# How the probabilities of the windowed attention are turned on TensorE in a hybrid block: by an fp32r copy and one-pass transposes, with q's and k's transposes as ordinary products

## The reference

```python
hn = rms_norm(h, mix_norm_g)
rq, rk, rv, rg, sq, sk, sv, gr, gs = split(hn @ w_in)
y_ret = rms_norm(retention(rq, rk, rv)) * silu(rg)
y_swa = sliding_window_attention(sq, sk, sv, q_norm_g, k_norm_g, sinks)
merged = sigmoid(gr) * (y_ret @ w_ret_branch) + sigmoid(gs) * (y_swa @ w_swa_branch)
h = h + merged @ w_out
h = h + square(relu(rms_norm(h, mlp_norm_g) @ w_up)) @ w_down
```

```python
scores = q @ keys.T - slopes * dist          # 128 x 272 a head and block
m = maximum(max(scores), sink)
p = exp(scores - m)
probs = p / (sum(p) + exp(sink - m))
y = probs @ vals
```

## Time and profile before

| what | us |
|---|---|
| median of three runs | 1619.83 |
| lowest and highest | 1619.79, 1620.44 |
| span of the profiled execution, first to last instruction | 1618.2 |
| median less that span | 1.6 |
| TensorE busy (share of the span) | 1610.1 (99%) |
| VectorE busy | 1030.6 (64%) |
| ScalarE busy | 769.9 (48%) |
| GpSimd busy | 437.1 (27%) |

### The profile page before, as it was taken

One profiled execution on the slowest core, in us unless ns is written; L12 is line 12 of the kernel. 1 busy time (PEld: TensorE's weight loads), 2 busy tenths in 40 slices (PEclk: granted clock), 3 DMA queues, 4 the chain that ended last, 5 costly groups with the idle time before them and its releaser, 6 DMA issues.

```text
span 1618.2 us, 22594 instructions
## 1 busy us (share of the span) xinstructions
PE 1610.1 (99%) x7984; PEld 1347.5 (83%) x7984; DVE 1030.6 (64%) x1913; ACT 769.9 (48%) x1567; POOL 437.1 (27%) x675
## 2 busy tenths in 40 slices
PE   9999999999999999999999999999999999999999
PEld 6888888888888888888888888888888888888887
DVE  6775556655657676757565338866665657766675
ACT  6533334545547676763222126655545544444442
POOL 1101010221359888875221000121111122100000
PEclk9999999999999999999999999999999999999999
DMA  8323232645424343438553223344444399733452
GB/s 289 116 98 117 95 124 72 232 166 186 162 88 114 84 94 83 106 82 262 164 202 104 72 65 124 129 170 150 149 144 148 119 321 356 239 98 98 149 183 92
DMA packets 119599, 236.53 MB, mean 146 GB/s; under 512 B 13904, under 2 KB 48128, under 8 KB 119488
## 3 DMA queue, kind: packets, MB, share of 16 engines
q0 software_dynamic: 45904, 126.93, 23.6%
q1 hardware_dynamic: 73440, 108.03, 21.6%
q10 hardware_dynamic: 144, 0.13, 0.0%
HBM read 157.05 MB, written 69.47 MB: 140 GB/s over the span
## 4 chain that ended last, share of the span: by engine, by line
PE 97%; DVE 1%; DMA 1%; ACT 0%; SPq 0%; POOL 0%; issue 0%; DVEq 0%; ACTq 0%
PE bank L1084 29%; PE bank L1089 29%; PE bank L1088 29%; PE bank L1370 2%; PE bank L1402 2%; PE bank L1384 2%; PE bank L1419 0%; PE bank L1127 0%; PE bank L1502 0%; PE bank L1288 0%; PE bank L1406 0%; PE bank L1452 0%; DMA PX<-in_w_in 0%; PE bank L1387 0%; DVE WL L2172 0%; PE bank L1427 0%
## 5 line engine op out<-in xcount | busy, mean ns | idle before, releaser
L1084 PE MATMUL bank<-WH,ADH 128*128 128x512 f32 x448 | 174.3, 389 | 0.0
L1088 PE MATMUL bank<-WH,ADL 128*128 128x512 f32 x448 | 174.3, 389 | 0.0
L1089 PE MATMUL bank<-WL,ADH 128*128 128x512 f32 x448 | 174.3, 389 | 0.0
L1084 PE MATMUL bank<-HN,WH 128*128 128x512 f32 x384 | 152.4, 397 | 0.0
L2098 ACT CAST ADH<-ARAW 128x512 fp32r<-128x512 f32 x112 | 69.5, 621 | 169.9 <-PE bank L1089 160.9
L1089 PE MATMUL bank<-HN,WH 128*128 128x512 f32 x384 | 150.3, 391 | 0.0
L1088 PE MATMUL bank<-HN,WL 128*128 128x512 f32 x384 | 150.0, 391 | 0.0
L959 POOL TENSOR_SCALAR PR<-PR,RC 128x272 f32<-128x272 f32 (+1 forms) x128 | 131.0, 1099 | 44.9 <-DVE RC L2663 44.4
L2917 DVE TENSOR_TENSOR ADL<-ARAW,ADH 128x512 fp32r<-128x512 f32 x112 | 77.5, 692 | 96.9 <-ACT ADH L2098 96.7
L1084 PE MATMUL bank<-SOPH,WH 128*128 128x512 f32 x256 | 99.8, 390 | 0.0
L1089 PE MATMUL bank<-SOPL,WH 128*128 128x512 f32 x256 | 99.6, 389 | 0.0
(11 more groups left out here) (356 smaller groups left out, 4242.8 us busy)
## 6 DMA issues: line engine op xcount, KB each, us to landing
ARAW<-uop SPq DMA_DIRECT2D x112, 256.0 KB, 3.0
uop<-US POOLq DMA_DIRECT2D x64, 256.0 KB, 2.8
WRAW<-in_w_up SPq DMA_DIRECT2D x15, 1024.0 KB, 6.2
RAW<-in_w_in SPq DMA_DIRECT2D x58, 256.0 KB, 4.0
gates<-TB POOLq DMA_DIRECT2D x48, 256.0 KB, 2.4
uop<-UA POOLq DMA_DIRECT2D x48, 256.0 KB, 3.1
proj<-SA POOLq DMA_DIRECT2D x36, 256.0 KB, 2.5
RT<-proj POOLq DMA_DIRECT2D x8, 1024.0 KB, 8.8
```

The costliest lines, as they stand in the source:

```text
L1084: mm = pe.matmul(bank, ahi, bhi, start=first, stop=False, skip_group_check=onto)
L1088: pe.matmul(bank, alo, bhi, start=False, stop=False, skip_group_check=onto)
L1089: return pe.matmul(bank, ahi, blo, start=False, stop=last, skip_group_check=onto)
```

## The change

- A new tile PW (fp32r, two buffers of 128 x 544) takes a copy of the pair's probabilities. SP makes it by a DMA (`copy_p`), which waits until GpSimd has scaled the pair (pn_rdy) and the pair before the last in this buffer is turned.
- The turn reads PW with IDR, an fp32r transpose instead of an fp32 one (what the change calls one-pass), and comes a step later: LAG = 3 instead of 2, STEPS 68 instead of 67. The values move from even to odd steps.
- q's and k's turns, in the loop and ahead of it, are no transposes any more but ordinary products with IDR. In the loop they are no longer a group behind P's turn: each stands by itself between two of the last gate products of its step (`turn_next`, through a callback `between` in `three`), so ahead of the values, P's turn and the scores.
- The sinks are written by VectorE at the head of `top`, which now waits for the copy of pair T - 3 and not for its turn.
- PW takes room: KV holds four token blocks instead of eight, K/V are loaded later, and the two aside weight blocks have a tile of their own (RAWA). Loads of weight blocks 2, 3, 6 and 7 are issued two steps later; those that follow blocks 0 and 1 stay.

```diff
+LAG = 3
-STEPS = NPAIR + 3
+STEPS = NPAIR + LAG + 1
...
+        PW = at("PW", O_M + 12288, [2, 2 * NKEY], F32R)
...
+            def copy_p(pair):
+
+                n, b = pair // 8, pair % 2
+                lo, hi = (0, 2 * NKEY) if n else (P, P + 2 * NKEY0)
+                sp.wait_ge(pn_rdy, pair + 1)
+                if pair >= 2:
+                    sp.wait_ge(pt_full, pair - 1)
+                sp.dma_start(PW[:, b, lo:hi].bitcast(F32), PR[:, pair % 3, 1 + lo:1 + hi]).then_inc(pw_full[b], 16)
+
             for T in range(STEPS):
+                if 2 <= T < NPAIR + 2:
+                    copy_p(T - 2)
+                if T >= LAG + 2 and T % 2 == 1:
+                    G = (T - LAG - 2) // 2
+                    sp.wait_ge(ya_rdy, G + 1)
+                    for par in range(2):
+                        sp.dma_start(y_place(G, par), y_part(G, 0, par)).then_inc(yc_done[G % 2], 16)
...
                 for slab, k in new_slabs(T):
                     if slab < SLAB_E and k in (0, 1):
                         load_next(slab, k + 6, (slab, k))
-                    elif slab < SLAB_E and k not in (4, 5):
+                for slab, k in new_slabs(T - 2) if T >= 2 else ():
+                    if slab < SLAB_E and k not in (0, 1, 4, 5):
                         load_next(slab + 1, (k + 2) % 8 if k > 5 else k, (slab, k))
...
-            def three(bank, ahi, alo, bhi, blo, first, last, frees, onto=False):
+            def three(bank, ahi, alo, bhi, blo, first, last, frees, onto=False, between=None):
 
                 mm = pe.matmul(bank, ahi, bhi, start=first, stop=False, skip_group_check=onto)
...
+                if between:
+                    between(0)
                 pe.matmul(bank, alo, bhi, start=False, stop=False, skip_group_check=onto)
+                if between:
+                    between(1)
                 return pe.matmul(bank, ahi, blo, start=False, stop=last, skip_group_check=onto)
...
             def transpose_p(pair):
-                n, b = pair // 8, pair % 3
-                pe.wait_ge(pn_rdy, pair + 1)
+                n, b = pair // 8, pair % 2
+                pe.wait_ge(pw_full[b], PW0 + 16 * (pair // 2 + 1))
...
-                        pe.transpose(B[4][:, c * P:(c + 1) * P], PR[:, b, key:key + P], IDN[:, :])
+                        pe.transpose(B[4][:, c * P:(c + 1) * P].bitcast(F32R), PW[:, b, key:key + P], IDR[:, :])
...
-                for j in range(4):
-                    mm = pe.transpose(B[5][:, j * P:(j + 1) * P].bitcast(F32R), q_rows(4 * g + j), IDR[:, :])
-                mm.then_inc(aq_full, 1)
...
+                mm = pe.matmul(B[5][:, j * P:(j + 1) * P], q_rows(4 * g + j), IDR[:, :], start=True, stop=True)
+                if j == 3:
+                    mm.then_inc(aq_full, 1)
...
+            def turn_next(T, c):
+
+                j = c - (3 * len(gate_steps(T)) - 4)
+                if T in NEXT_Q and j >= 0:
+                    turn_next_q(*NEXT_Q[T], j)
+                if T in NEXT_K and 0 <= j < 2 * len(NEXT_K[T][1]):
+                    turn_next_k(*NEXT_K[T], j)
 
             for T in range(STEPS):
                 for i in gate_steps(T):
-                    gate_step(i)
-                if T >= 4 and T % 2 == 0:
-                    values((T - 4) // 2)
-                if 2 <= T < NPAIR + 2:
-                    transpose_p(T - 2)
-                if T in NEXT_Q:
-                    transpose_next_q(*NEXT_Q[T])
-                if T in NEXT_K:
-                    transpose_next_k(*NEXT_K[T])
+                    gate_step(i, lambda c, at=3 * (i - gate_steps(T).start): turn_next(T, at + c))
+                if T >= LAG + 2 and T % 2 == 1:
+                    values((T - LAG - 2) // 2)
+                if LAG <= T < NPAIR + LAG:
+                    transpose_p(T - LAG)
                 if T < NPAIR:
                     scores(T)
...
                 if T >= 3:
-                    dve.wait_ge(pt_full, T - 2)
+                    dve.wait_ge(pw_full[(T - 3) % 2], PW0 + 16 * ((T - 3) // 2 + 1))
...
+                dve.tensor_copy(PR[:, T % 3, first:second + 1:second - first], NSK[:, 2 * p:2 * p + 2]).then_inc(sk_set, 1)
```

More of the change, by code:

```diff
@@ L589, in raw_block @@
                 return RAW[:, place, :] if place < 4 else RAWE[place - 4][:, :]
[L590 to L591 removed]
+            if k in (4, 5) and slab in ASIDE:
+                return RAWA[:, k - 4, :]
             return RAWE[k - 4][:, :] if k >= 4 and slab == SLAB_E and RA_E else RAW[:, raw_slot(slab, k), :]
@@ L1087, in three, with step @@
                     mm.then_inc(w_free, 1)
+                if between:
+                    between(0)
                 pe.matmul(bank, alo, bhi, start=False, stop=False, skip_group_check=onto)
+                if between:
+                    between(1)
                 return pe.matmul(bank, ahi, blo, start=False, stop=last, skip_group_check=onto)
-            def step(form, bank, k, f, act, slab, opening, closing):
+            def step(form, bank, k, f, act, slab, opening, closing, between=None):
                 if opening:
@@ L1100, in step @@
                     fs = slice(f * P, (f + 1) * P)
-                    mm = three(bank[:, :], WH[:, w, fs], WL[:, w, fs], hi, lo, k == 0, k == KT - 1, frees)
+                    mm = three(bank[:, :], WH[:, w, fs], WL[:, w, fs], hi, lo, k == 0, k == KT - 1, frees, between=between)
                 else:
@@ L1319, in transpose_k @@
                     for g in range(4):
-                        mm = pe.transpose(B[2 + part][:, g * rows:(g + 1) * rows].bitcast(F32R),
-                                          KST[0:rows, part, g, :], IDR[0:rows, 0:rows])
+                        mm = pe.matmul(B[2 + part][:, g * rows:(g + 1) * rows], KST[0:rows, part, g, :],
+                                       IDR[0:rows, 0:rows], start=True, stop=True)
                     mm.then_inc(ak_full, 1)
@@ L1349, in gate_step @@
                     pe.wait_ge(a_free, ACT_D + i // 8 - 1)
-                mm = step("S", B[q % 2], k, q, hn_half(s), SLAB_D + i // 64, s == 0 and q == 0, s == 1 and q == 3)
+                mm = step("S", B[q % 2], k, q, hn_half(s), SLAB_D + i // 64, s == 0 and q == 0, s == 1 and q == 3,
+                          between=between)
                 if k == KT - 1:
                     mm.then_inc(a_full, 1)
+                if between:
+                    between(2)
             ahead = {18: transpose_meta_k, 25: transpose_new_k, 28: transpose_q}
@@ L1410, in values, with turn_next_q @@
                 mm.then_inc(pv_full, 1)
[L1412 to L1417, removed]
-                for j in range(4):
-                    mm = pe.transpose(B[5][:, j * P:(j + 1) * P].bitcast(F32R), q_rows(4 * g + j), IDR[:, :])
-                mm.then_inc(aq_full, 1)
[L1422 to L1428, removed]
-                    mm.then_inc(ak_full, 1)
+            def turn_next_q(m, g, j):
+                if j == 0:
+                    pe.wait_ge(ql_rdy, 3 * m + 1)
+                    if g == 3:
+                        pe.wait_ge(aqT_rdy, 4 * m + 3)
+                    else:
+                        pe.wait_ge(akT_rdy, 4 * m + g)
+                mm = pe.matmul(B[5][:, j * P:(j + 1) * P], q_rows(4 * g + j), IDR[:, :], start=True, stop=True)
+                if j == 3:
+                    mm.then_inc(aq_full, 1)
@@ new lines, in turn_next_k @@
+            def turn_next_k(m, gs, j):
+                if j == 0:
+                    pe.wait_ge(ql_rdy, 3 * m + 2)
+                    pe.wait_ge(aqT_rdy, 4 * m + 4 if len(gs) > 1 else 4 * m + gs[0] + 1)
+                g, part = gs[j // 2], j % 2
+                mm = pe.matmul(next_k(g)[:, part * P:(part + 1) * P], KST[:, part, g, :], IDR[:, :], start=True, stop=True)
+                if part == 1:
+                    mm.then_inc(ak_full, 1)
+            def turn_next(T, c):
[4 more added lines that the diff above has]
+                    turn_next_k(*NEXT_K[T], j)
```

106 lines of the change are left out of this document (47 added, 59 removed).

## The result

| | before | after |
|---|---|---|
| median, us | 1620.13 (4 runs, 1619.79 to 1620.78) | 1634.40 (4 runs, 1632.43 to 1637.39) |
| profiled execution: span, its own time | 1618.2 | 1630.4, 1632.43 |
| ratio | | 1.009, 95% interval 1.0077 to 1.0103 |

The account below looks back on a forecast made before the run. TensorE bounds the kernel (97% of the chain, busy 59.5 of 60 us). -4.7 + 3.0 + 0.5 + 1.0 + 0.3 = +0.1 us on the 1618.2 span, 1.6 under the median: forecast 1620.0, range 1612 to 1625.5.

Parts of the forecast that it names:

- P's turns: TensorE's turns of P in the loop as fp32r: a bunch of five 0.47 us instead of 0.55, gaining 4.7 us.
- The copy on SP: SP's 64 transfers into PW: landing 3.3 us, 4.9 available, spare 1.3, so hidden; 1 us in all (0 to 4).
- Rival B: The copy into PW comes late as a rule: 28 pairs about 1.2 us late, +34, 1654 us; chance 0.08.
- Its weak form: The copy into PW comes 0.3 us late in 28 pairs: +8, 1628 us.
- The slab changes: At three slab changes SP's copy stands behind block 7's load, awaiting block 1's split: 0.3 us each, 1 in all.
- The woven products: q's and k's 168 loop turns as single products between gate products: 0.112 us each, 18.8 against 15.8, losing 3.0 us.
- rival A: Woven products in the loop are cheap: 0.058 us each, -6.1 instead of +3.0; 1611 to 1615.6 us; chance 0.25.
- QT: q's first woven product wants ScalarE's QT some 2.5 us earlier, just in time: 0.3 us for the loop (0 to 5).
- The products ahead of the loop: 16 q and 8 k turns ahead of the loop as products at 0.112 us each: a loss of 0.5 us.
- The sinks, one step more, K/V: Sink copies moved to VectorE, one more loop step, later K/V loads: nothing on TensorE.

Follow-up runs that it names:

- experiment 1: The kernel before with only P's turns made fp32r, read from P's own memory, no copy: 1614.37 us beside 1619.84.
- 8: The changed kernel without the copy, P turned from its own memory, and q's and k's loop turns back as grouped fp32r transposes: 1614.07 us.
- 3: The changed kernel with P turned from its own memory and the copies not issued; q's and k's products still woven: 1619.93 us.
- experiment 2: The changed kernel with the copies still issued but not read by TensorE, which turns P from its own memory: 1621.87 us.
- experiment 5: The changed kernel with the loads of a slab's weight blocks 6 and 7 issued one step later, behind the copy: 1637.80 us.
- 7: The changed kernel with blocks 6 and 7 loaded one step later, RAWE loads five steps later and distance loads four steps later: 1631.39 us.
- experiment 6: The changed kernel with the four RAWE weight loads five steps later and the distance loads four steps later: 1627.67 us.

## Why the prediction was wrong

**The account of the 14.3 us**, in steps of measured medians: P's turns as fp32r -5.5 (experiment 1); the rest of the change without copy and without weaving -0.3 (8 less 1); q's and k's woven products with their waits +5.9 (3 less 8); the copies issued but not waited for by TensorE +1.9 (2 less 3); waiting for the copy +12.5 (after less 2). Sum +14.5, beside the 14.3 measured; the steps come from three sittings whose runs of before differ by 0.3.

- **The step that failed** is "The copy on SP": "The spare is 1.3 us: hidden" and "1 us in all (0 to 4)". It cost 14.4 us, 12.5 waiting and 1.9 otherwise. I had compared one typical landing, 3.3 us, with one typical slack, 4.9. The median was right at 3.1, and the typical slack no smaller than the 4.9 that I had taken (its median over the 64 pairs is 6.1). But landing (2.0 to 6.6 us), the delay of the issue (up to 3.7 us) and the slack (3.8 to 6.9 us in the pairs that waited) vary each by itself, and TensorE pays for the tail: a pair that is early gives nothing back, one that is late is paid in full. Even the row of the slowest loads at 4.8 lies under five of the six landings that were too slow: it was measured with the DMA engines at a share of 0.40 to 0.45, and the copies themselves raised that to 0.6. Rival B put that figure into every second pair or into none; what took place is nine pairs at 0.4 to 2.4 us. Its weak form, 1628, had the right kind of mechanism and too little size.
- **The slab changes** were foreseen in place (three of them, copy behind block 7's load) and mis-sized: 3.1 us of waits against 1. I had put the issue of the middle one 3.05 us ahead of its turn (568.2 to 571.25), from the load at 567.88 in the kernel before; in the changed kernel it went out 1.5 us ahead (571.20, wanted at 574.40 - 1.71 = 572.69), behind two loads.
- **P's turns**: -4.7 forecast, -5.5 measured. From the first turn to the scores 616.85 - 616.45 = 0.40 us, as I had written. Right.
- **The woven products**: +3.0 forecast. Each is 0.34 less 0.23, as forecast, so rival A is out. The total is 4.4 (5.9 less 1.5 of waits on QT), because the grouped turns that they replace cost 0.086 and not the 0.094 that I had divided out of a group behind fp32 turns: once P's turns are fp32r too, the whole group runs at the quicker pace, 168 x 0.113 - 168 x 0.086 = 4.5. I had compared the new product with the old turn and not with the turn as the same change would have left it; part of the 0.8 us by which P's turns beat their forecast is this quicker pace of q's and k's turns behind them. The Trainium skill (TensorE: Matmul & The Clock Gate, Back-to-back issue gap) has 81 ns for such a product; the 0.113 and 0.117 here disagree. The estimate of 107 ns by the rule for loads in the same page's section LDWEIGHTS is the nearer one. (Worked out from it, P's gain is 56 x (0.55 - 0.535) = 0.8 us and not the 0.6 that the prediction gives; nothing else hung on it.)
- **QT**: 0.3 forecast (0 to 5), 1.5 without the copies and 3.5 with them unread: in the range and too low. In the changed kernel itself it shows nothing, as the copy's waits hide it. In experiments 5 and 7 it came back with 2.8 and 2.9.
- **The clock** was not in the sum at all. Behind some waits of about 2 us TensorE ran at 1.2 GHz for some 3.4 us, about 1.5 us lost each time; by the mean clocks of the runs that is some 3 of the 14.3 us at the median. The sizes are read from the traces, not separated by a run.
- **The products ahead of the loop**: +0.5 forecast, +0.6 by the rows. Right.
- **The sinks, one step more, K/V**: nothing forecast; with the products ahead -0.3, nothing that can be told.

**Open.** Of experiment 6's 6.7 us, 4.0 are waits on the copy and about 1.5 the clock; 1 us is unexplained, as between the spans of after and experiment 2. Why some waits of about 2 us bring the lower clock and others don't, no run shows. Nor what makes pair 8's landing slow. And no version was tried in which the copy is issued by another queue than SP's.

## What to carry to other kernels

Before you add a transfer to a loop, compare its slowest landing, at the share of the DMA engines that the loop will have with it, with the smallest slack; the medians hide it, and the queue's waits ahead of it (here a weight split on VectorE) count as part of the landing. Ask whether the copy is needed at all: here the same fp32r turn reads the tile where it lies, and that one edit, 5.5 us, is all the gain there was. And when a change touches two kinds of work that stand in one group, price the second against the group as the first leaves it.

## What the runs showed of the hardware

- A block of fp32 probabilities turned as fp32r straight from its memory costs 0.085 us in a group, as fp32 0.11; the same turn written as an ordinary fp32r product costs 0.113 between long products and 0.117 in a group. Being woven between products of 512 columns saves it nothing.
- Transfers of up to 272 KB within SBUF landed in 2.0 to 6.6 us in one execution; moving ten other transfers away from them took the maximum to 5.4. Beside them GpSimd's y stores of 64 KB landed in 4.0 us (median) instead of 3.2.
- After a wait of 2.07 us TensorE's products of 512 columns went 0.43 us apart for some 3.4 us (1.2 GHz) and then 0.23 again, at a cost of about 1.5 us; after one of 2.41 us in the same execution they didn't. In experiment 5 it happened three times, behind waits of 2.5, 2.8 and 2.5 us.
